# Order of the two token halves inside a matmul slab of a hybrid encoder step

## The reference

```python
for i in range(DEPTH):
    h = rmsnorm(x, norm_mix[i])
    if i % 2 == 0:
        u, v, z, xbc, dt_raw = split(h @ l0_w_in)           # 1024 -> 4624 columns
        ya = gmlp_mix(u, v, ...); yb = mamba_mix(z, xbc, dt_raw, ...)
        x = x + concat([ya, yb]) @ l0_w_out                 # 2048 -> 1024
    else:
        x = x + retention_mix(h, ...)                       # 1024 -> 6144, 2048 -> 1024
    h = rmsnorm(x, norm_ffn[i])
    x = x + (silu(causal_dwconv(h @ w_gate)) * (h @ w_up)) @ w_down     # 1024 -> 2816 -> 1024
    gate = sigmoid(rmsnorm(x, norm_ple[i]) @ ple_w_gate[i])
    x = x + gate * (p[i] @ ple_w_proj[i])                   # 256 -> 1024
return rmsnorm(x, norm_final), and the new states
```

## Time and profile before

| | |
|---|---|
| median of 3 runs | 1935.55 us (1934.4 to 1935.87) |
| profiled execution | 1934.12 us |
| its span, first to last instruction | 1932.3 us |
| mean granted TensorE clock | 0.972 |
| PE busy | 1837.8 us, 95% |
| DVE, ACT, POOL busy | 949.2, 629.0, 861.5 us |

### The profile page before, as it was taken

The page is one execution under the profiler, slowest core; times in us unless marked ns, Lnnn a source line. Parts: engine busy times, 40 slices in busy tenths (PEclk is TensorE's granted clock), DMA queues, the critical chain, the costliest instruction groups (busy, mean ns, idle before and its releaser), DMA issues.

```text
span 1932.3 us, 34346 instructions
## 1 busy us (share of the span) xinstructions
PE 1837.8 (95%) x14081; PEld 1779.9 (92%) x14081; DVE 949.2 (49%) x1526; ACT 629.0 (33%) x913; POOL 861.5 (45%) x431
## 2 busy tenths in 40 slices
PE   5969989899999999999899999999799999999996
PEld 5969977799999999999899999999699999999996
DVE  4264765556652452455644443344455524525555
ACT  5333422234322222234433332233234422222342
POOL 3352332246554454456543333433155544544562
PEclk8989979899999999999999999999899999999998
DMA  5212211012233222223222222222112222232221
GB/s 211 77 44 69 77 44 44 23 55 88 88 110 132 88 87 99 85 68 109 77 80 75 79 79 76 85 79 75 52 65 77 88 97 88 87 99 82 66 95 46
DMA packets 49472, 156.76 MB, mean 81 GB/s; under 512 B 5984, under 2 KB 10208, under 8 KB 49376
## 3 DMA queue, kind: packets, MB, share of 16 engines
q1 hardware_dynamic: 43200, 145.57, 21.7%
q10 hardware_dynamic: 6176, 9.83, 1.5%
HBM read 149.75 MB, written 5.63 MB: 80 GB/s over the span
## 4 chain that ended last, share of the span: by engine, by line
PE 87%; DVE 8%; ACT 2%; issue 1%; DMA 1%; POOL 0%; SPq 0%; DVEq 0%; POOLq 0%; ACTq 0%
PE proj L316 78%; PE Q L926 7%; DVE arena L1659 1%; ACT arena L623 1%; DVE rstd L366 1%; DVE op_lo L386 1%; DMA w_raw<-in_w_v 1%; DVE arena L1510 0%; ACT op_hi L373 0%; DVE arena L1326 0%; PE Q L1159 0%; DVE v_tok L1416 0%; DVE x L1661 0%; PE proj L926 0%; DVE arena L1284 0%
## 5 line engine op out<-in xcount | busy, mean ns | idle before, releaser
L411 POOL TENSOR_TENSOR w_lo<-w_raw,w_hi 128x1024 fp32r<-128x1024 f32 (+2 forms) x276 | 651.6, 2361 | 785.4 <-ACT w_hi L337 785.0
L316 PE MATMUL proj<-op_hi,w_hi 128*128 128x256 f32 x4288 | 899.8, 291 | 28.6 <-DVE op_lo L386 18.6
L316 PE MATMUL proj<-op_hi,w_lo 128*128 128x256 f32 x4288 | 891.1, 289 | 0.0
L316 PE MATMUL proj<-op_lo,w_hi 128*128 128x256 f32 x4288 | 884.4, 288 | 0.0
L316 PEld LDWEIGHTS proj<-op_hi,w_hi 128*128 128x128 f32 x4288 | 690.4, 190 | 38.8 <-issue 16.3
L316 PEld LDWEIGHTS proj<-op_lo,w_hi 128*128 128x128 f32 x4288 | 693.2, 190 | 0.0
L316 PEld LDWEIGHTS proj<-op_hi,w_lo 128*128 128x128 f32 x4288 | 688.5, 189 | 0.0
L337 ACT ACTIVATE w_hi<-w_raw 128x1024 fp32r<-128x1024 f32 (+2 forms) x276 | 284.7, 1032 | 731.6 <-PE proj L316 727.6
L1326 DVE TENSOR_TENSOR arena<-proj,rstd 128x512 f32<-128x512 f32 x145 | 100.1, 691 | 232.6 <-PE proj L316 197.8
L1333 DVE TENSOR_TENSOR x<-proj,x 128x512 f32<-128x512 f32 x72 | 49.8, 692 | 261.6 <-PE proj L316 261.6
L926 PE MATMUL Q<-arena 128*128 128x256 f32 (+9 forms) x524 | 119.3, 378 | 11.4 <-DVE arena L1520 7.5
(11 more groups left out here) (159 smaller groups left out, 1017.3 us busy)
## 6 DMA issues: line engine op xcount, KB each, us to landing
w_raw<-in_w_gu SPq DMA_DIRECT2D x88, 512.0 KB, 3.2
w_raw<-in_w_down SPq DMA_DIRECT2D x32, 512.0 KB, 3.2
w_raw<-in_w_heads_a SPq DMA_DIRECT2D x30, 512.0 KB, 3.3
w_raw<-in_w_heads_b SPq DMA_DIRECT2D x18, 512.0 KB, 3.2
w_raw<-in_w_gate SPq DMA_DIRECT2D x16, 512.0 KB, 3.2
w_raw<-in_w_xbc SPq DMA_DIRECT2D x12, 512.0 KB, 3.2
w_raw<-in_w_down SPq DMA_DIRECT2D x16, 384.0 KB, 3.0
w_raw<-in_w_v SPq DMA_DIRECT2D x8, 512.0 KB, 8.0
```

The costliest lines, as they stand in the source:

```text
L316: last = nc.tensor.matmul(proj[:, 2 * g.mod(2) + half, 0:size], w[:, lo:lo + P], o[:, at:at + size], start=(k == 0 and j == 0), stop=(k == ...
L411: nc.gpsimd.tensor_tensor(w_lo[:, c:c + width], w_raw[:, c:c + width], w_hi[:, c:c + width], ALU.subtract).then_inc(w_lo_done, 1)
```

## The change

The loop over the two token halves, which was the innermost of the slab, becomes the outermost. A slab issues the low half (256 tokens) for all operand tiles and all passes, and then the high half (288 tokens) for all of them. The waits on `ready` are issued in the first half alone, once for each operand tile as before. The number of matmuls and their operands, the flags of the accumulation, the wait on `tile_read` at the start and the count on `tile_done` at the last matmul are the same.

```diff
-                for k in range(ph.kt):
-                    if ready:
-                        pe.wait_ge(ready[0], ready[1] + k)
-                    lo = slot * SLAB + (k * ph.m + m) * P
-                    passes = ((w_hi, op_hi[ops]), (w_hi, op_lo[ops]), (w_lo, op_hi[ops]))
-                    for j, (w, o) in enumerate(passes):
-                        for half in range(2):
-                            size = HALF if half == 0 else HALF + TS
-                            at = (k0 + k) * T + half * HALF
+                for half in range(2):
+                    size = HALF if half == 0 else HALF + TS
+                    for k in range(ph.kt):
+                        if ready and half == 0:
+                            pe.wait_ge(ready[0], ready[1] + k)
+                        lo = slot * SLAB + (k * ph.m + m) * P
+                        at = (k0 + k) * T + half * HALF
+                        passes = ((w_hi, op_hi[ops]), (w_hi, op_lo[ops]), (w_lo, op_hi[ops]))
+                        for j, (w, o) in enumerate(passes):
                             last = nc.tensor.matmul(proj[:, 2 * g.mod(2) + half, 0:size], w[:, lo:lo + P],
                                                     o[:, at:at + size], start=(k == 0 and j == 0),
                                                     stop=(k == ph.kt - 1 and j == 2))
```

## The result

The new order takes 1975.26 us in the median of 4 runs (1973.78 to 1976.43), before 1934.97 us: a ratio of 1.0208, 95% interval 1.019 to 1.0226, so it is slower by about 2%. The forecast was 1971.2 us, within 1959 to 1985. The profiled execution has a span of 1973.9 us against 1932.3, 41.6 us more.

What follows compares the result with a forecast made beforehand. The prediction took PE, with a matmul in flight for 95% of the span, as the bound. Starved first slabs, 27.7 us, and clock falls, 8 us, with steady slabs at 0, gave 1971.2 us, range 1959 to 1985.

Steps and rivals of the forecast that it cites:

- v: First slab of v: PE waits for late tiles and the clock rises late, costing 3.8 us, bounds 2.5 and 4.1.
- heads_a: First slab of heads_a, already starved and at the lower clock: slab 1 ends at 974.05 instead of 971.5, 2.5 us.
- Starvation: First slabs of dependent phases: high-half matmuls move behind the last tile's landing at 0.13 us each, 27.7 us in all.
- The clock: PE's new idle stretches: 3.5 falls of the granted clock at 2.3 us, 8 us; bounds none and 24 us.
- The steady slabs: Steady slabs: same 48 matmuls and 48 weight loads, 6.00 us as before, so a change of 0.
- Rival C: All matmuls: accumulating into one bank back to back stalls, 150 us more, 2120 us; chance 0.05.
- rival E: All matmuls: a small loss or gain each beside A's 36 us, taking it out of A's bounds; chance 0.04.
- A: Whole kernel, likeliest case: starved first slabs plus clock falls, 36 us more, 1962 to 1988 us; chance 0.82.
- The sign that the prediction set itself: Steady slabs: the prediction is wrong if one differs from 6.00 us by more than 0.1 us.
- B: All matmuls: alternating banks costs 11.7 ns each today, so 150 us would go, about 1822 us; chance 0.05.
- D: Waits in first slabs: PE takes high-half matmuls past the waiting one, so no change, 1935.5 us; chance 0.04.

Runs made afterwards that it cites:

- e7: Kernel before, with the new order for only the last four operand tiles of a slab: 1949.86 us against 1935.07, ratio 1.0073.
- e6: New order, with idle stretches ahead of late tiles in v, outb, downs and heads_a filled with overwritten matmuls: 1965.91 us, ratio 1.0165 to before.
- e8: Kernel before, with each operand tile's three low passes issued first, then its three high ones: 1936.18 us against 1935.07, ratio 1.0005.
- e2: Kernel before, with the new order only in slabs given a ready wait, the old order elsewhere: 1972.31 us, ratio 1.0203.
- e5: New order with the low half widened to 288 columns, the 32 extra computed and not read: 2064.71 us, run once.

## Why the prediction was right, and where it was off

The first slab of each dependent phase, from its first matmul to the next slab's, before and after, beside the terms of the forecast (us). "Low" is time at the lower clock with PE at work that was not there before.

| | forecast | measured | low |
|---|---|---|---|
| v | 3.8 | 14.45 − 10.44 = 4.0 | the clock rose at 23.70 |
| outb | 2.4 | 11.80 − 8.00 = 3.8 | 3.41 |
| gu00 | 2.25 | 8.97 − 6.69 = 2.3 | 0 |
| down00, down01 | 2.73 each | 4.1, 4.2 | 3.41 each |
| down02 | 1.95 | 8.33 − 4.89 = 3.4 | 3.41 |
| heads_a | 2.5 | 16.71 − 13.48 = 3.2 | 0.6 |
| gu10 | 2.0 | 8.71 − 6.69 = 2.0 | 0 |
| down10 | 2.73 | 10.41 − 6.18 = 4.2 | 3.41 |
| down11 | 2.73 | 8.87 − 6.18 = 2.7 | 0 |
| down12 | 1.95 | 6.81 − 4.86 = 1.95 | 0 |
| ret_b | 0 | 7.69 − 8.06 = −0.4 | less |

- *Starvation.* Where the clock stayed up (gu00, gu10, down11, down12) the terms hold to 0.05 us. The rule that made them, moved matmuls × 0.13 us less the time by which the tile was early, was confirmed in the downs by the dose of e7. The column of measured values sums to 35.6 us; five falls at 1.5 us taken out, 28 us stay against 27.7. In heads_a the clock was low for 4.71 us of work behind the landing instead of 4.08, which is some 0.3 us of the 0.7 that the term lacks. In v the forecast had the clock low for 5 us behind 18.63; the distance of matmuls went from 0.24 to 0.13 us at 23.70.
- *The clock.* The forecast was 3.5 falls at 2.3 us, 8 us; there were five at 1.5 us, 7.5 us. Both factors were off and their product right, which is luck. The price comes from the pair down10 and down11, one idle for 2.61 us, the other for 2.59, then 10.41 and 8.87 us for the same slab. The figure of 2.3 had been taken from slabs that began at the lower clock and stayed there for some 5.4 us, not 3.41. e6 gave 9.4 us back: by its first slabs 7.3 us in the five phases with a fall, 1.3 in v and 0.8 in heads_a.
- *The steady slabs.* This is the step that failed: "the same 48 matmuls with the same 48 weight loads ... so 0". It is 0.04 us a slab, by the traces 10.7 us over 268 slabs' worth of matmuls. The nearest rows, transposes at half the column rate, could not show an effect of 0.8 ns per matmul. Rival C (stalls) had it only at the size of the whole 11.7 ns; rival E had a small loss per matmul beside A's, but as a way out of A's bounds and not as a term of the sum. The sign that the prediction set itself, 0.1 us a slab, was too coarse to catch it: 0.1 us over 268 slabs would be 27 us.
- *What made the total fit.* Starvation 28, falls 7.5, steady slabs 10.2 outside the first slabs, together 46; of it some 3.5 us came back elsewhere, which no step claims. outa, low for 27.3 instead of 34.1 us, is 2.6 us shorter than its surplus would have it, heads_b, low for 13.6 instead of 19.5 us, 0.5 us, and u, at the same 17.1 us low, 0.4 us. That gives 42 against the span's 41.6 us. The median came out 4 us over the forecast: a missing term of 10 us is hidden in part behind this luck and the scatter between an execution and the median. outa before and after, the whole phase:

```profile
244.13:394.12 149.99, 129.53 (x856) 0.89 0.10 34
```

```profile
248.44:396.16 147.72, 126.53 (x856) 0.91 0.11 34
```

- *The rivals.* B (faster) and D (no change) are out by the steady slab and by the gaps. The surplus per matmul over the columns' time is there in both orders, 11.4 ns in gu01 before and 12.2 after, so alternating the banks is not its cause. The 2.5 ns above the columns' time that the Trainium skill gives ("TensorE: Matmul & The Clock Gate", "Back-to-back issue gap") are met by neither order. But the section gives them for a matmul by itself and says that in a stream in which each matmul has its own weight load, both set the distance. These kernels are such a stream, so the disagreement that rival B rests on is weaker than the prediction has it.

Nothing here beats the kernel before. e8 equals it.

## What to carry to other kernels

In a slab that consumes tiles as they are produced, what counts is how much work stands ahead of the wait for the last tile. Keep every piece of work that needs only earlier tiles ahead of it: each matmul that a loop order moves behind the landing is paid in full as soon as the tile was just in time, and here the old order had hidden 5.4 us of latency behind 42 matmuls to within 0.2 us in down00. Before such a loop is turned, look at how close the landing is to the need; and count the clock, too: here it fell at five of the nine new idle stretches of 1.7 to 3.3 us, for 1.5 us each.

## What the runs showed of the hardware that was not expected

The granted clock after nearly equal idle stretches went either way, and it fell after work had resumed. Windows of PE around the resumption, of down10 (idle, work at the full clock, work at the lower), then down11 (idle, work):

```profile
1583.36:1585.97 2.61, 0.00 (x1) 1.00 0.00 0
1585.97:1587.00 1.03, 1.03 (x8) 1.00 0.51 103
1587.01:1590.42 3.41, 3.41 (x16) 0.50 0.36 127
1732.41:1735.00 2.59, 0.00 (x1) 1.00 0.31 39
1735.00:1738.64 3.64, 3.64 (x27) 1.00 0.75 270
```

PE had been at work for a microsecond when the clock went down for 3.41 us. down02's idle stretch of 2.03 us was followed by a fall, down12's of 2.03 us was not. In e2 it was the other way about between other phases, its down11 at a mean clock of 0.83 over the first slab, its down02 at 1.00:

```profile
872.98:879.84 6.86, 4.77 (x38) 1.00 0.20 57
1725.03:1735.20 10.17, 7.54 (x50) 0.83 0.36 119
```

e5 is a third trace of the new order in these slabs, with shorter idle stretches, as its matmuls are wider. down00 there, idle and then at work, and the idle stretch of down02, behind which the clock stayed up:

```profile
626.73:628.73 2.00, 0.00 (x1) 1.00 0.36 70
629.60:633.01 3.41, 3.41 (x17) 0.50 0.93 238
915.07:916.52 1.45, 0.00 (x2) 1.00 0.00 0
```

Of the nine phases outb, down00, down01 and down10 had a fall in all three traces (outb for 6.83 us in e2 and e5), down11 in two, down02 in one, and gu00, gu10 and down12 in none. The length of the idle stretch alone does not decide: 2.00 us led to a fall in e5 and 2.59 us to none in down11 after. So a single fall can't be told from the phase for certain; a count over many phases is what can be forecast.
